# Moving 27 modulation tiles of a two-block kernel into its gating stage, folded to one chunk by the vector engine

## The reference

```python
m_x = (silu(c) @ w_mod + b_mod).reshape(6, 1024)      # modulation: 48 output chunks of 128 columns
hx  = rmsnorm(x, g1) * (1 + m_x[1]) + m_x[0]          # chunks 0 to 15, the first norm ("moda")
px  = hx @ w_in                                       # rx, rg (1280), u, v, gr, gg (1024)
y_r = gelu(rg) * (recurrence both ways over rx, gates by w_a and w_x)
y_g = gelu(u) * (per-head mix of the normed gelu(v) over tokens)
x   = x + m_x[2] * ((sigmoid(gr) * (y_r @ w_pr) + sigmoid(gg) * (y_g @ w_pg)) @ w_out)
h2  = rmsnorm(x, g2) * (1 + m_x[4]) + m_x[3]
x   = x + m_x[5] * ((gelu(conv2d(h2 @ up_g)) * (h2 @ up_l)) @ w_down)   # chunks 16 to 47 are m_x[2] to m_x[5]
x   = rmsnorm(x, g_final)
# second block: a state-space branch and forgetting attention, gated and projected, then a layer
# that takes 16 of 16384 experts for each of 8 heads (w_u, w_v tables of 128 tiles each)
```

## Time and profile before

| | us |
|---|---|
| median of 3 runs | 3299.36 |
| lowest, highest | 3298.22, 3299.91 |
| the profiled execution | 3299.58 |
| its span, first to last instruction | 3297.8 |
| TensorE busy | 3206.1 (97%) |
| DVE busy | 2051.5 (62%) |
| ACT busy | 1246.7 (38%) |
| POOL busy | 430.4 (13%) |

### The profile page before, as it was taken

One profiled execution on the slowest core, in us unless ns is written; L12 is line 12 of the kernel. 1 busy time (PEld: TensorE's weight loads), 2 busy tenths in 40 slices (PEclk: granted clock), 3 DMA queues, 4 the chain that ended last, 5 costly groups with the idle time before them and its releaser, 6 DMA issues.

```text
span 3297.8 us, 37501 instructions
## 1 busy us (share of the span) xinstructions
PE 3206.1 (97%) x14140; PEld 2526.4 (77%) x14140; DVE 2051.5 (62%) x3404; ACT 1246.7 (38%) x2289; POOL 430.4 (13%) x188
## 2 busy tenths in 40 slices
PE   7999999989989899999989999999999999999999
PEld 6877778868868665667668888888888888888887
DVE  5678443348898788636734898677771455555554
ACT  4266232223223322134433233999993211111111
POOL 0000000004123000000001354333334000000000
PEclk9999999999999999999999999999999999999999
DMA  5144324322242333222122344668777555555553
GB/s 201 56 136 134 99 74 140 117 96 83 76 148 80 131 125 112 79 75 71 39 77 95 129 138 140 172 178 219 189 211 227 195 191 192 185 186 190 192 189 111
DMA packets 280964, 451.56 MB, mean 137 GB/s; under 512 B 147784, under 2 KB 154056, under 8 KB 280528
## 3 DMA queue, kind: packets, MB, share of 16 engines
q1 hardware_dynamic: 145168, 405.12, 37.0%
q10 hardware_dynamic: 135616, 44.04, 5.9%
HBM read 369.39 MB, written 79.69 MB: 136 GB/s over the span
## 4 chain that ended last, share of the span: by engine, by line
PE 89%; DVE 8%; ACT 1%; issue 1%; DMA 0%; POOL 0%; ACTq 0%; DVEq 0%
PE psum L599 89%; DVE psum L1751 1%; DVE wl L1398 1%; ACT wh L995 1%; DVE trigw L1495 0%; DVE yb L1609 0%; DVE trig L1496 0%; DVE trig L1491 0%; DVE trig L1494 0%; DVE trig L1493 0%; DVE trigw L1492 0%; DVE lb L1600 0%; DVE cs L1607 0%; DVE y L1611 0%; DVE n L1534 0%
## 5 line engine op out<-in xcount | busy, mean ns | idle before, releaser
L599 PE MATMUL psum<-h_hi,wh 128*128 128x512 f32 x2144 | 858.8, 401 | 45.3 <-DVE wl L1398 16.1
L1398 DVE TENSOR_TENSOR wl<-ring,wh 128x1024 fp32r<-128x1024 f32 (+2 forms) x320 | 373.4, 1171 | 789.4 <-ACT wh L995 788.5
L599 PE MATMUL psum<-h_lo,wh 128*128 128x512 f32 x2144 | 850.7, 397 | 0.0
L599 PE MATMUL psum<-h_hi,wl 128*128 128x512 f32 x2144 | 850.4, 397 | 0.0
L995 ACT ACTIVATE wh<-ring 128x1024 fp32r<-128x1024 f32 (+2 forms) x492 | 504.4, 1027 | 826.6 <-PE psum L599 806.1
L2106 POOL TENSOR_TENSOR wl<-ring,wh 128x1024 fp32r<-128x1024 f32 x172 | 427.6, 2487 | 1817.4 <-ACT wh L995 1817.4
L599 PEld LDWEIGHTS psum<-h_hi,wh 128*128 128x128 f32 x2144 | 407.3, 190 | 146.9 <-issue 54.2
L599 PEld LDWEIGHTS psum<-h_hi,wl 128*128 128x128 f32 x2144 | 406.8, 190 | 95.7
L599 PEld LDWEIGHTS psum<-h_lo,wh 128*128 128x128 f32 x2144 | 407.3, 190 | 88.8 <-issue 1.9
L599 PE MATMUL psum<-ews_hi,wh 128*128 128x512 f32 x1024 | 404.1, 395 | 0.7 <-ACT ga L1365 0.7
L599 PE MATMUL psum<-ews_hi,wl 128*128 128x512 f32 x1024 | 404.0, 395 | 0.0
(11 more groups left out here) (374 smaller groups left out, 3815.8 us busy)
## 6 DMA issues: line engine op xcount, KB each, us to landing
ring<-tables SPq DMA_DIRECT2D x256, 512.0 KB, 3.6
acts_scratch<-ga SPq DMA_DIRECT2D x128, 256.0 KB, 2.2
gates_scratch<-stage ACTq DMA_DIRECT2D x8, 4096.0 KB, 25.3
abuf<-acts_scratch SPq DMA_DIRECT2D x128, 256.0 KB, 3.8
gbuf<-gates_scratch SPq DMA_DIRECT2D x128, 256.0 KB, 4.0
ring<-w_up SPq DMA_DIRECT2D x44, 512.0 KB, 3.5
ring<-w_modb SPq DMA_DIRECT2D x32, 512.0 KB, 3.5
statew<-states_scratch SPq DMA_DIRECT2D x16, 640.0 KB, 3.7
```

What stands on the lines that cost most here:

```text
L599: return nc.tensor.matmul(out, lhsT, rhs, start=first, stop=last, **kw)
L1398: TT(wl, slot(t, 0, size[t]), wh.bitcast(F32), ALU.subtract).then_inc(S("low_by_ve"), 1)
```

## The change

- Modulation. 27 of the 32 `modb` tiles (`MODB_LATE`) move from the gate stage into the gating, into 27 of 32 places (`MODB_AT`; the places 6, 12, 19, 25 and 31 stay empty). There DVE multiplies the tile by silu(c) and adds its eight chunks to one in three halving steps (`fold_modulation`), and TensorE needs one matmul of 16 columns against ones. The last five tiles stay as they were, at 64 columns, and run behind `out7`.
- In the gating, halves are made up to R = 5 tiles ahead instead of 3, if the slot of the half isn't still in use after tile t; `low_of_modulation` and `high_of_modulation` do so at the places of the moved tiles too.
- Orders: the first four `moda` tiles run before the column sums and are loaded before x, which comes in two parts; the lows of `rg3` and `rg4` are placed between the last scans; DVE's lows between the `yg` products are spread; `out0` and `out1` are projected together, chunk by chunk; halves behind `out7`, `down1_7` and `out2_7` come after the last addition to x; in the last two `vo` tiles the banks are finished one by one, so that DVE's additions can start earlier.
- Sums. In `out` and `out2` DVE adds the squares of chunks 0 to 6, and TensorE sums two columns' worth instead of eight. At the double norm the scale of the second square is sqrt(g_final^2 + eps), which replaces two DVE steps.
- The lows of `g12` and `l11` are made by DVE instead of POOL. Several semaphore chains are merged into one.

The diff, cut to its core:

```diff
-MA, MB = 64, 64
-MODB = [32 * n // (2 * NR) for n in range(2 * NR + 1)]
+MA, MB, MS = 64, 64, 16
+MODB_LATE = 27
+MODB_AT = {4 * n + k: [] for n in range(KD) for k in range(4)}
+for _k in range(MODB_LATE):
+    MODB_AT[32 * _k // MODB_LATE].append(_k)
...
-    for _k in range(MODB[_n], MODB[_n + 1]):
-        stage(f"modb{_k}", ["T"], False)
...
 stage("mix", ["B"] * (HG - 1) + ["BT"], False, lambda k: ("yg_mixed", k + 1))
...
+def folded_modulation(i):
+    for k in MODB_AT[i]:
+        stage(f"modb{k}", ["T"], False)
...
     stage(f"gr{_u}", ["BT"], True, lambda k, u=_u: ("gr_tanh", u + 1))
+    folded_modulation(4 * _u)
...
     stage(f"pr{_u}", ["T", "BT"], True, lambda k, u=_u: ("pr_mul", u + 1))
+    folded_modulation(4 * _u + 1)
     stage(f"gg{_u}", ["BT"], True, lambda k, u=_u: ("gg_tanh", u + 1))
+    folded_modulation(4 * _u + 2)
...
     stage(f"pg{_u}", ["BT"], True, lambda k, u=_u: ("pg_mul", u + 1))
+    folded_modulation(4 * _u + 3)
...
     stage(f"out{_u}", ["BT"], True, lambda k, u=_u: ("x_mixed", u + 1))
+for _k in range(MODB_LATE, 32):
+    stage(f"modb{_k}", ["T"], False)
...
         FFN += [f"down{_n // NFH}_{_u}" for _u in range(KD)]
+FFN_BY_GP = [name for name in FFN if name[0] != "d" and name not in ("g12", "l11")]
...
-modb = psum[:, 4:8, :].rearrange("p b (n r) -> p (b n) r", r=MB)
+modb = psum[:, 4, :].rearrange("p (n r) -> p n r", r=MB)
+mods = psum[:, 6, :].rearrange("p (n r) -> p n r", r=MS)
...
     sp.dma_start(vec[:, :], io["vecs"]).then_inc(S("vecs_loaded"), 16)
...
     for u in range(16):
+        if u == 4:
+            for k in range(2):
+                sp.dma_start(xc[:, 4 * k:4 * k + 4, :], io["xc"][:, 4 * k:4 * k + 4, :])\
+                    .then_inc(S(f"x_loaded{k}"), 16)
...
         fetch(TILE[f"gates{n}"], io["w_gates"][n], 4 * P)
-        for k in range(MODB[n], MODB[n + 1]):
-            fetch(TILE[f"modb{k}"], io["w_modb"][k])
...
+    def fetch_modulation(i):
+        for k in MODB_AT[i]:
+            fetch(TILE[f"modb{k}"], io["w_modb"][k])
...
         fetch(TILE[f"gr{n}"], io["w_gr"][n])
+        fetch_modulation(4 * n)
...
             fetch(TILE[f"pr{n}"] + k, io["w_pr"][n][:, 5 * P * k:5 * P * (k + 1)], 5 * P)
+        fetch_modulation(4 * n + 1)
         fetch(TILE[f"gg{n}"], io["w_gg"][n])
+        fetch_modulation(4 * n + 2)
...
         fetch(TILE[f"pg{n}"], io["w_pg"][n])
+        fetch_modulation(4 * n + 3)
...
     stream("out", "w_out", KD)
+    for k in range(MODB_LATE, 32):
+        fetch(TILE[f"modb{k}"], io["w_modb"][k])
...
             mm(psum[:, bk, :], ones[:, :], nrm[k][n % 2], c == 0, c == KD - 1).then_inc(S("sq_used"), 1)
+    def folded_sums(k, first, bk, roots, rest):
...
+        if rest:
+            pe.wait_ge(S("sq_ready"), first + KD)
+            mm(psum[:, bk, :], ones[:, :], nrm[k][1], False, True).then_inc(S("sq_used"), 1)
+        else:
+            pe.wait_ge(S("sd_done"), roots)
+            pe.wait_ge(S("sq_used"), first + KD - 2)
+            mm(psum[:, bk, :], ones[:, :], nrm[k][3], True, False).then_inc(S("sq_used"), 1)
...
+    def late_modulation(n):
...
+        t, at = TILE[f"modb{n}"], (n - MODB_LATE) * MB
+        tile_here(pe, t)
+        for k in range(KD):
+            last = mm(psum[:, 4, at:at + MB], wchunk(t, k), silu_c[:, k:k + 1].to_broadcast([P, MB]), k == 0,
+                      k == KD - 1)
+        last.then_inc(PE, 1)
...
         for n in range(KD + 2):
-            if n < KD:
+            if stage == "out" and n < 2:
+                if n == 0:
+                    project_two(("out0", "out1"), kw["act"], kw["ready"], 0)
+            elif n < KD:
...
                 project(f"{stage}{n}", ready.pop("act"), **ready)
-            if n >= 2:
+            if len(banks) == 2 and n >= 2:
                 column_sums(k, first, banks, roots, n - 2)
+            if len(banks) == 1 and n >= KD:
+                folded_sums(k, first, banks[0], roots, n == KD + 1)
+            if stage == "out" and n == KD - 1:
+                late_modulation(MODB_LATE)
+        if stage == "out":
+            for n in range(MODB_LATE + 1, 32):
+                late_modulation(n)
...
+    def first_modulation(u):
...
+        if u % 2 == 0:
+            wait(pe, S("mod_read"), u // 2 - 3)
+        modulation(f"moda{u}", psum[:, 4 + u // 2 % 4, u % 2 * 2 * MA:(u % 2 + 1) * 2 * MA], 2 * MA)
+    pe.wait_ge(S("silu_ready"), KD + 1)
+    for u in range(4):
+        first_modulation(u)
...
         mm(psum[:, 1, 0:TC], ones[:, :], sq[:, T:TX], c == 0, c == KD - 1).then_inc(S("sq_used"), 1)
-    pe.wait_ge(S("silu_ready"), KD)
-    for u in range(16):
-        if u % 2 == 0:
-            wait(pe, S("mod_read"), u // 2 - 3)
-        modulation(f"moda{u}", psum[:, 4 + u // 2 % 4, u % 2 * 2 * MA:(u % 2 + 1) * 2 * MA], 2 * MA)
+    for u in range(4, 16):
+        first_modulation(u)
...
+    def folded_modulation(i):
...
+        for k in MODB_AT[i]:
+            pe.wait_ge(S("mod_folded"), k + 1)
+            mm(psum[:, 6, MS * k:MS * (k + 1)], wchunk(TILE[f"modb{k}"], 0), ones[:, 0:MS], True, True)\
+                .then_inc(PE, 1)
...
         project(f"gr{n}", h)
+        folded_modulation(4 * n)
...
         project(f"pr{n}", yr, ready="yr_ready" if n == 0 else None, parts=(5, 5))
+        folded_modulation(4 * n + 1)
         project(f"gg{n}", h)
+        folded_modulation(4 * n + 2)
...
         project(f"pg{n}", ygs, ready="yg_ready" if n == 0 else None)
+        folded_modulation(4 * n + 3)
...
         halves_here(pe, e)
-        for kk in range(2):
+        if half == 0:
+            pe.wait_ge(S("ew_ready"), 2 * m + 1)
+        order = [(kk, c) for kk in range(2) for c in range(4)]
+        if m == PK // 2 - 1:
+            order.sort(key=lambda o: o[1])
+        for kk, c in order:
             b = 2 * m + kk
-            if half == 0:
+            if half == 0 and kk == 1:
                 pe.wait_ge(S("ew_ready"), b + 1)
-            for c in range(4):
-                last = three(psum[:, 4 * half + c, :], whl(e, 4 * kk + c), ews, b % NV,
-                             b == 0, b == PK - 1)
+            last = three(psum[:, 4 * half + c, :], whl(e, 4 * kk + c), ews, b % NV, b == 0, b == PK - 1)
+            if m == PK // 2 - 1 and kk == 1 and c < 3:
+                last.then_inc(S("out_summed"), 1)
...
     A(s_cos, sc[2], ACT.Sin).then_inc(S("s5_act"), 1)
...
         A(hc[0][:, c, :], xc[:, c, T:TX], ACT.Identity, bias=mod[:, c, 1:2]).then_inc(S("h_high"), 1)
-        if c == KD - 3:
+        if c == 3:
...
         act.dma_start(states_d[c][:, 2 * T:SW], bt[:, c % 2, :]).then_inc(S(f"bt_parked{c % 2}"), 16)
+    def high_of_modulation(i):
+        for k in MODB_AT[i]:
+            high_after(TILE[f"modb{k}"], R)
...
             A(mt[:, 2 * (n % 2) + j, :], bank(b), ACT.Tanh, scale=0.5).then_inc(S(f"{name}_tanh"), 1)
-            high_after(TILE[f"{name}{n}"])
+            high_after(TILE[f"{name}{n}"], R)
+            high_of_modulation(4 * n + 2 * j)
             input_map(2 * n + j)
-            high_after(TILE[f"map{2 * n + j}"])
+            high_after(TILE[f"map{2 * n + j}"], R)
...
             if j == 0:
-                high_after(TILE[last])
-                high_after(TILE[last] + 1)
+                high_after(TILE[last], R)
+                high_after(TILE[last] + 1, R)
             else:
-                high_after(TILE[last])
+                high_after(TILE[last], R)
+            high_of_modulation(4 * n + 2 * j + 1)
...
         act.wait_ge(S("x_mixed"), n + 1)
-        wait(act, S("sq_used"), KD + n - 1)
-        A(nrm[1][n % 2], x[:, n, :], ACT.Square).then_inc(S("sq_ready"), 1)
+        wait(act, S("sq_used"), KD + max(n - 2, 0))
+        A(nrm[1][n % 2 if n else 3], x[:, n, :], ACT.Square).then_inc(S("sq_ready"), 1)
     root(1, 2 * KD)
+    high_after(TILE["modb30"])
...
                     wait(act, S("sq_used"), k - 1)
-                    A(nrm[2][k % 2], x[:, n, :], ACT.Square, scale=C("gfin", n) if j else 1.0)\
+                    A(nrm[2][k % 2], x[:, n, :], ACT.Square, scale=gfe[:, n:n + 1] if j else 1.0)\
                         .then_inc(S("sq_ready"), 1)
...
-    def low_after(t):
...
-        while next_low[0] < HALF[TILE["ui0"]] and WHOLE_OF[next_low[0]] <= t + RH:
+    def low_after(t, ahead=RH):
...
+        while next_low[0] < HALF[TILE["ui0"]] and WHOLE_OF[next_low[0]] <= t + ahead:
+            if ahead > RH and WHOLE_OF[next_low[0] - RH] > t:
+                break
...
                 TT(y[:, c, :], y[:, c, :], yb, ALU.add).then_inc(S("lru_done"), 1)
+            if g == 3 and j in (1, 3):
+                low_after(TILE[f"rg{j // 2}"])
     ve.wait_ge(S("lru_done"), 2 * NR)
-    tile_used(ve, TILE["modb31"])
-    TT(mod[:, 16:48, 0:1], modb[:, :, 0:1], bm[:, 16:48, 0:1], ALU.add).then_inc(S("mod_read"), 1)
-    ve.wait_ge(S("mod_read"), KD + 1)
-    link(TS(hm2, mod[:, 16:24, 0], 0.5, None, ALU.mult))
-    link(STT(a2, mod[:, 32:40, 0], 1.0, V("g2"), ALU.add, ALU.mult))
```

(78 more changed lines are left out.)

83 lines of the change are left out of this document (46 added, 37 removed).

## The result

The changed kernel takes 3307.84 us (median of 15 runs, 3304.69 to 3310.82) against 3298.35 us (15 runs, 3296.94 to 3299.91): the ratio is 1.0029, with an interval from 1.0021 to 1.0037. It is slower by 0.29 per cent, just past the 0.2 per cent that the prediction took as the least that can be told from no change. The forecast was 3296 with more chance on faster than on slower; the time is inside the range of 3258 to 3320, but on the other side of no change.

A forecast was written before the change was run, and what follows sets the result against it. The prediction took TensorE's matmul to bound the kernel nearly everywhere, with pauses at joins. Its terms -30 -10 +64.6 -13.1 -5.7 -5.4 -2 -1.9 gave -3.5, so 3296 us; eight-in-ten range 3258 to 3320.

The forecast's parts named there:

- a sum of -68 and +65: Whole kernel: gains expected everywhere outside the gating, set against the gating's expected loss of +64.6 us; net -3.5.
- the join at the first norm: Between out7 and the feed-forward part: g1's low ready at 12.0 us against 9.5, clock stays up (-1.9): +0.6 us.
- Start, -10: Before rx: four moda tiles run before the column sums while x loads, rx starts near 48: -10 us (-7 to -11).
- Gate stage, -30: Recurrence gates to sixth rg tile: modb matmuls leave, DVE and ACT limit next: -30 us (-20 to -36).
- Rival 2: Gate stage doesn't gain: half clock lasts through both units after the scans, giving 31 us back: 3327 us; chance 0.15.
- Gating, +64.6: Gating stage: DVE and ACT stand until TensorE frees a folded tile's slot and the next lands: +64.6 us (+13 to +75).
- Out and first norm, -13.1: Out tiles through first norm: out0 and out1 together -8.5, six column sums fewer -5.2, join +0.6: -13.1 us.
- g12, l11, -2: Feed-forward part: DVE instead of POOL makes these two lows: -2 us, bounds -6 and +4.
- Second norm -5.4: Join at the second norm: u2's lows off the way, sum pair at full clock, two DVE steps fewer: -5.4 us.
- rest -7.6: After the second norm: out2's six sums and a low off the tail -5.7, hidden adds at the end -1.9 us.
- the first (folds hide): Gating stage: DVE's folds hide, blocked lows cost only 13 to 30 us: 3244 to 3261 us; chance 0.20.
- The third (half clock in the gating): Gating stage: half clock after every pause and some slower landings, +10 to +20, so 3306 to 3316 us; chance 0.15.

The follow-up runs named there:

- nine_in_gates: Changed kernel without early halves behind folds, slots freed by DVE, TensorE two places behind, g2's half earlier, 9 of 27 tiles back between gate units: 3238.92 us.
- the kernel without the stalls: Changed kernel without early halves behind folded tiles, slots freed by DVE, TensorE taking each folded chunk two places later: 3246.81 us, ratio 0.9841.

## Why the prediction was wrong

The direction hung on a sum of -68 and +65. The forecast was -3.5, the profiled execution came out at +7.2, and the 10.7 between them are +9.2 in `out` and the first norm, +6.7 in the gating, -3.2 in the gate stage and -2.0 in the rest. The step that failed is the join at the first norm. The sum gave it +0.6: 2.5 us more to wait and 1.9 of clock given back. It cost +8.7: 3.7 more to wait, no clock given back, and a pause at the third tile behind it that the sum didn't have. The second miss is the size of the gating, +71.3 instead of +64.6. Step by step:

- **Start, -10.** Right: `rx` at 48.16 us, forecast 48. The column sums take 10.56 us now instead of 13.47, and the slow stretch lies in the four tiles before them: 9.09 us for 64 matmuls, where the 192 behind the sums take 21.60, or 7.2 for 64. It shows in these rates alone; the profile lists a granted clock of 1.00 for both.

```profile
5.26 9.09 PE L626 MATMUL psum<-silu,ring 128*128 128x128 f32 x64 [5.26 <-ACT silu L1079]
14.73 10.56 PE L626 MATMUL psum<-n,ones 128*128 128x512 f32 x32 [0.39 <-ACT n L1098]
...
48.16 0.47 PE L626 MATMUL psum<-h_hi,wh 128*128 128x512 f32 x1 [1.43 <-DVE wl L1483]
```

- **Gate stage, -30.** Right in sum, with 3.2 more gained. The sixth `rg` tile starts at 303.47, 168.8 us after the first gate unit at 134.69 (forecast 168); 1.5 of the 3.2 lie before that unit, in `rx`. But half of the gain isn't the move's: with the 27 tiles left in their places the same stretch is 184.7 us (320.66 - 135.96), against 200.6 before. The pause of 8.3 us at an `rg` tile is 2.6 there, so the lows placed between the last scans have a part in it; they weren't tested alone. TensorE's clock is 0.50 behind the pauses of 4.4 us, and the 32 matmuls up to the next wait take 13.45 us, where the same 32 take 10.56 at full clock in `nine_in_gates`; yet TensorE waits again, for 0.7 us, before the next stretch at full rate, so the slow one was not on the path. Rival 2 put its price where DVE covers it.

```profile
170.22 13.45 PE L626 MATMUL psum<-xr,ring 128*128 128x512 f32 x32 [4.42 <-ACT rr L1133]
184.37 15.72 PE L626 MATMUL psum<-xr,ring 128*128 128x512 f32 x48 [0.69 <-ACT rr L1133]
...
303.47 0.47 PE L626 MATMUL psum<-h_hi,wh 128*128 128x512 f32 x1 [2.10 <-DVE wl L1483]
```

- **Gating, +64.6.** The chain was right in kind, place and almost in size (+71.3). The excess is in n = 1, 2 and 7 (2.3 + 2.6 + 1.7 = 6.6); the others cancel. In n = 1 the 2 MB load of x (issued at 480.47, 10.9 us to land) stands in the same queue, and two `modb` tiles issued around it took 6.2 and 5.3 us to land; whether that is the excess wasn't tested. For n = 2 and 7 the cause is open. What the forecast left unweighed is which of the causes that it named in one breath matters: it put the slot that TensorE frees first, and the experiments give this 9.5 us, but 37 to the request for the half right behind the fold, and 14 to TensorE's taking each fold in its place.
- **Out and first norm, -13.1.** This is the step that failed: -3.9. The `out` tiles gave 12.5 (57.5 to 45.0 us) of the 13.7 in the sum. But the join behind them took 13.3 us instead of 9.6, where the forecast had 2.5 more; the clock was 0.50 behind it again (760 to 762), so the 1.9 didn't come back; and a pause of 3.5 with its clock (5.0 in all) came at the third tile. The pause was a miss of counting: `high_after` behind `modb30` reaches three tiles, `modb31`, `g0` and `g1`, so the third feed-forward tile is out of reach until TensorE has done the first two. The longer join is in part the slow `h_lo` (1.6 us) beside POOL, in part ACT's copy of `g1`, which waits for its landing until 755.04 with the highs of the norm queued behind it. The forecast's path to the first matmul was the low of `g1`, ready 12.0 us behind `out7`; it was ready at 12.6 (758.52), but `h_lo`, at 759.07, ended the wait. The pauses:

```profile
759.21 0.47 PE L626 MATMUL psum<-h_hi,wh 128*128 128x512 f32 x1 [2.70 <-DVE h_lo L1632]
...
775.70 0.47 PE L626 MATMUL psum<-h_hi,wh 128*128 128x512 f32 x1 [3.54 <-POOL wl L2234]
...
968.43 0.47 PE L626 MATMUL psum<-h_hi,wh 128*128 128x512 f32 x1 [2.03 <-DVE wl L1483]
...
993.54 0.47 PE L626 MATMUL psum<-h_hi,wh 128*128 128x512 f32 x1 [2.56 <-POOL wl L2234]
```

- **g12, l11, -2.** It was -4.5 in the trace, 5.3 by the experiment. **Second norm -5.4, rest -7.6.** They were -5.6 and -7.0.

Of the rivals, the first (folds hide) was excluded by the changed kernel, yet it is what the kernel without the stalls does: DVE at 74 per cent of the stage (155.1 of 209.9 us) hides the folds. Its time, 3244 to 3261, is that of the experiments (3246.8). The third (half clock in the gating) holds in part: TensorE is busy 224.5 us in the stage, and 202.8 where it never waits for a fold, so slow clock costs some 22 us of the 71. But the forecast's own chain counts 2 us of clock behind each long pause; what it lacked in the stage is 6.7 at most. That the time fell into this rival's band, 3306 to 3316, is luck in part, since the larger excess lies at the first norm. The chances don't quite add up either: with each rival whole on its side they give 0.40 faster, 0.22 same and 0.38 slower, not 0.41, 0.24 and 0.35. By the rule of the Trainium skill that the prediction named ("TensorE: Matmul & The Clock Gate", section "HAM oscillation — how this bites in real kernels"), waits for a transfer between short runs of matmuls should bring the fall again and again; the trace agrees, the clock was at 0.50 behind the pause of 4.15 us at 574.05 and behind others of the stage.
